# Delta net of a fused two-block network: diagonal blocks gathered by GpSimd, the convolution's last tap on ScalarE, value tiles between the inverse's levels, another entry

## The chip, the cores and the metric

The kernel runs on one core of a Trainium2 chip. The metric is the device time of one execution in microseconds (us); three runs of the kernel before gave 2810.44, 2818.19 and 2819.06, median 2818.19. The engines are TensorE (PE in the profile), VectorE (DVE), ScalarE (ACT), GpSimd (POOL) and SyncE (SP, which only issues the weight transfers here). Each has its own instruction queue and they meet at semaphores. TensorE writes to PSUM, eight banks of 128x512 float32 values.

## The reference, cut to what matters

The network has a first block (two attention layers), and a second one: a feed-forward layer, a mixer and another feed-forward layer, all on 512 tokens of width 1024 in float32. The mixer has two branches. The change concerns one of them, the gated delta net, with 8 query/key heads, 16 value heads, width 128, in chunks:

```
qkv = silu(causal_short_conv(concat([gq, gk, gv]), conv_w))    # 4 taps along the tokens
q_g = l2norm(cq) * 128 ** -0.5;  k_g = l2norm(ck)               # repeated for 2 value heads each
beta = sigmoid(gb);  g = -exp(a_log) * softplus(ga + dt_bias);  gam = cumsum(g)
A  = where(strict, (beta k) k^T * exp(gam_t - gam_s), 0)
T  = inverse(I + A)                                             # unit lower triangular
qk = q k^T * exp(gam_t - gam_s)                                 # t >= s
per chunk:  v_new = T (beta v) - T (beta k exp(gam)) S
            o = (q exp(gam)) S + qk v_new
            S = S exp(g_end) + k_to_end^T v_new
o_g = rmsnorm(o) * silu(gz)
```

## The kernel before, in words

The kernel is a hand-written program: for each engine a Python function issues instructions in a fixed order, and explicit semaphore waits tie the queues together. Nothing reorders them. The delta net works in four groups `g` of two query/key heads and four value heads. A token tile `j` (four of 128 tokens) and a value head give one of 16 units of a group, for which a 128x128 unit triangular matrix is inverted.

Per group there are two parts. `pe_gdn_prepare` and its namesakes on the other engines take the norms of q and k (`sums`: matmuls with one column of output, L2301), scale them (`scale`, L2310), form decays (`diff`, L2348) and products (`kq`, L2323 and L2324), and turn the value tiles 0 and 1 (`v_tok`, a transposition, L386). VectorE forms `lower` (A) and `qk` in four steps j (L3044 to L3057), convolves value tiles 4 and 5, and then solves the 32x32 diagonal blocks of all 16 units at once. For that it copies the blocks with four transposes (L3086), one for each band of 32 partitions, into `bm`, eliminates in 31 steps of two instructions (L3095, L3097), and turns the result back (L3099 gives `block`, L3101 `block_t`). Then it convolves the tiles 6 and 7.

`pe_gdn_inverse_and_state` builds the 128x128 inverse from the solved blocks in two levels: `x5` (L2360), `t5` and `r5` (L2370, L2376) for the 64 level, `x6` (L2385) and `r6` (L2395) for the 128 level, each evicted in halves by ScalarE and VectorE. GpSimd places the diagonal blocks into `tt` and `rr` (L3181, L3185). Value tiles 2 and 3 are turned behind `x5` and behind `r5`. Then come four steps of the state: `ks` and `qs` (L2413, L2418), `vn` (L2430, evicted as `v_new` by ScalarE, L2733), `su` (L2438) and `do` (L2444).

Between all this, TensorE takes steps of a `fill` stream: projections that do not depend on the group, one matmul of 512 columns a step, eight steps a tile, four tiles of `gv`, of `gz` and of the next `gqk` for each group (L2216 and L2234). Each float32 matmul appears as two records in the trace. The fill uses the banks 6 and 7 in turn (`FILL_BANKS`); a bank is free again when ScalarE has copied the tile out. `LEAD` = 12 steps are taken ahead of a group.

A convolution of 4 taps along tokens goes tile by tile. ScalarE copies the projection from PSUM into `pad` behind three zero columns (`act_gdn_pad`, L2615), VectorE multiplies by tap 0 and adds taps 1, 2 and 3 (`dve_gdn_conv`: L3005, L3008 twice, L3010) into `acc`, ScalarE applies Silu (L2628). Both buffers are double, so pad `c` waits for convolution `c - 2`.

At the entry TensorE projects the first `gqk` into `HIGH_BANKS` (4 to 7), computes `gam` (L2259 to L2261), and starts the fill. VectorE zeroes `rr` and `tt` (2048 and 1024 columns, L2983 and L2986) and reduces the identity to `halves` (L2984) before its first convolution. ScalarE does the four Squares (L2637) after the last Silu.

## Time and profile before

| | |
|---|---|
| median of 3 runs | 2818.19 us (2810.44 to 2819.06) |
| profiled execution, its own time | 2815.83 us |
| its span, first to last instruction | 2814.0 us |
| PE busy | 2725.4 us |
| DVE busy | 1305.1 us |
| ACT busy | 620.5 us |
| POOL busy | 28.9 us |
| mean granted TensorE clock | 0.979 |

The delta net lies between about 1654 and 2234 us, in four groups of some 135 us. PE is busy when at least one matmul is under way; the ends of matmuls are modelled, so successive rows overlap by 0.1 to 0.2 us, and the distance from one row's start to the next's is the better price. "Idle before" in square brackets is the time that an engine stood before an instruction, and the name behind the arrow the instruction that released it. The granted clock is a share of 2.4 GHz; 0.5 is 1.2 GHz.

### The profile page before, as it was taken

Reading aid. Unit: us, or ns where it says so; the run is one execution under the profiler, and the core shown is the slowest. Engines: PE = TensorE matmul, PEld = TensorE weight load, DVE = VectorE, ACT = ScalarE, POOL = GpSimd, SP = SyncE. Lnnn points to the kernel's source line nnn. Section 1 sums busy time; section 2 is a strip of 40 time slices with the busy share of each in tenths; the row PEclk is TensorE's granted clock in tenths of the full one; section 3 lists DMA queues with packets and bytes.
Section 4 is the critical chain, followed back from the end, with each engine's and each line's share of the span. In section 5 each row is a group of like instructions: output and inputs, shape, how many; then the busy total and the mean of one; then the engine's idle time right before and its main releaser. Section 6 shows DMA issues by size and latency. Waiting matters only on the chain.

```text
span 2814.0 us, 29186 instructions
## 1 busy us (share of the span) xinstructions
PE 2725.4 (97%) x11644; PEld 1820.0 (65%) x11644; DVE 1305.1 (46%) x2545; ACT 620.5 (22%) x1428; POOL 28.9 (1%) x49
## 2 busy tenths in 40 slices
PE   8999899999999999999999989999999999999999
PEld 5445557656478888746555845646565685688886
DVE  3723333445234456335364427475756362344564
ACT  2122321346200000223333022424232201100001
POOL 0000000000000000000000000000000000000000
...
DMA packets 122478, 195.16 MB, mean 69 GB/s; under 512 B 7212, under 2 KB 63336, under 8 KB 121448
## 3 DMA queue, kind: packets, MB, share of 16 engines
...
q14 instruction: 41, 0.34, 0.0%
...
## 4 chain that ended last, share of the span: by engine, by line
PE 88%; DVE 8%; issue 1%; ACT 1%; DMA 1%; ACTq 0%; DVEq 0%; SPq 0%
PE psum L503 19%; PE psum L500 14%; PE psum L2234 10%; PE psum L413 9%; PE psum L433 8%; PE psum L2216 6%; PE psum L398 6%; PE psum L1137 2%; PE psum L2097 2%; PE psum L1157 2%; DVE arena L3097 1%; DVE arena L3095 1%; PE psum L631 1%; PE psum L1145 1%; PE psum L386 1%
## 5 line engine op out<-in xcount | busy, mean ns | idle before, releaser
L2234 PE MATMUL psum<-weight_ring,h_t 128*128 128x512 f32 x896 | 408.1, 598 | 0.5 <-issue 0.5
L556 DVE TENSOR_TENSOR arena<-arena,psum 128x512 f32<-128x512 f32 x179 | 122.8, 686 | 337.1 <-PE psum L503 287.7
L2234 PEld LDWEIGHTS psum<-weight_ring,h_t 128*128 128x128 f32 x896 | 162.7, 191 | 163.3 <-issue 162.1
L413 PE MATMUL psum<-h_t,weight_ring 128*128 128x512 f32 x560 | 246.7, 601 | 7.7 <-DMA weight_ring<-in_w_in_dram 4.0
L2216 PE MATMUL psum<-h_t,weight_ring 128*128 128x512 f32 x512 | 244.7, 621 | 8.4 <-ACT arena L2615 8.1
L503 PE MATMUL psum<-h_t,weight_ring 128*128 128x256 f32 x1024 | 228.2, 379 | 0.0
L500 PE MATMUL psum<-weight_ring,arena 128*128 128x256 f32 x992 | 220.2, 379 | 1.5 <-ACT arena L2647 1.5
L503 PEld LDWEIGHTS psum<-h_t,weight_ring 128*128 128x128 f32 x1024 | 194.5, 190 | 27.5 <-issue 1.3
L500 PEld LDWEIGHTS psum<-weight_ring,arena 128*128 128x128 f32 x992 | 188.4, 190 | 27.7 <-issue 2.2
L413 PEld LDWEIGHTS psum<-h_t,weight_ring 128*128 128x128 f32 x560 | 107.2, 193 | 142.7 <-issue 134.5
L398 PE MATMUL psum<-weight_ring,h_t 128*128 128x512 f32 (+3 forms) x512 | 182.9, 513 | 0.8 <-DVEq L1583 0.8
L433 PE MATMUL psum<-weight_ring,h_t 128*128 128x512 f32 x384 | 171.3, 608 | 3.3 <-ACT h_t L1224 2.0
L2216 PEld LDWEIGHTS psum<-h_t,weight_ring 128*128 128x128 f32 x512 | 97.4, 200 | 106.8 <-issue 105.6
L500 PE MATMUL psum<-arena 128*128 128x256 f32 x712 | 158.7, 379 | 0.0
L503 PE MATMUL psum<-arena 128*128 128x256 f32 x704 | 155.5, 379 | 0.0
L500 PEld LDWEIGHTS psum<-arena 128*128 128x128 f32 x712 | 135.3, 190 | 18.4
L398 PEld LDWEIGHTS psum<-weight_ring,h_t 128*128 128x128 f32 x512 | 92.8, 207 | 82.7 <-issue 81.6
L503 PEld LDWEIGHTS psum<-arena 128*128 128x128 f32 x704 | 133.8, 190 | 18.2
L433 PEld LDWEIGHTS psum<-weight_ring,h_t 128*128 128x128 f32 x384 | 74.5, 195 | 96.5 <-issue 94.9
L990 ACT ACTIVATE arena<-arena 128x1024 f32<-128x1024 f32 x20 | 21.2, 1058 | 421.3 <-DVE arena L556 421.3
L1173 ACT ACTIVATE arena<-arena,statistics 128x128 f32<-128x128 f32 (+1 forms) x96 | 53.9, 562 | 231.5 <-DVE statistics L1202 231.4
L503 PE MATMUL psum<-arena,weight_ring 128*128 128x256 f32 x384 | 86.8, 379 | 0.0
...
## 6 DMA issues: line engine op xcount, KB each, us to landing
...
```

Of the source, the lines that this page charges most:

```text
L398: last = pe.matmul(bank[:, 0:n_cols], act[:, k0 + k, t * P:(t + 1) * P], slot[:, k, col:col + n_cols], start=(k == 0), stop=(k == nk - 1))
L413: last = pe.matmul(bank, slot[:, k, c:c + P], act[:, k, :], start=(k == 0), stop=(k == KD - 1))
L433: last = pe.matmul(bank, act[:, k0 + k, t * P:(t + 1) * P], slot[:, k, :], start=(k == 0), stop=(k == nk - 1))
L500: ins = pe.matmul(out, right[:, k, q * P:(q + 1) * P], left[:, k, :], start=first, stop=last)
L503: ins = pe.matmul(out, w, right[:, k, :], start=first, stop=last)
L556: ins = dve.tensor_tensor(out, other, bank, op)
L1137: pe.matmul(bank[:, 0:k.shape[-1]], q, k, start=True, stop=True).then_inc(K.full_of((tag, "s", m)), 1)
L1157: last = pe.matmul(bank[:, 0:v.shape[-1]], probs_t[:, i % 2, kb * P:(kb + 1) * P], v, start=(kb == 0), stop=(kb == nkb - 1))
L1173: act.activation(probs[:, n % 2, 0:nk], masked[:, n % 2, 0:nk], ACT.Exp, bias=K.stat[:, 20 + n % 4:21 + n % 4], scale=steps[n]["scale"], a ...
L2097: last = pe.matmul(bank[:, j * P:(j + 1) * P], left[:, c], right[:, c], start=True, stop=True)
L2216: last = pe.matmul(bank, slot[:, k, n * P:(n + 1) * P], act[:, k, :], start=(k == 0), stop=(k == KD - 1))
L2234: last = pe.matmul(bank, act[:, k, t * P:(t + 1) * P], slot[:, k, :], start=(k == 0), stop=(k == KD - 1))
```

## The change

- The diagonal blocks are first copied side by side into a new tile `diag` by GpSimd, 16 copies of 32x128 per group, four for each step j as soon as `lower` of that step is there. VectorE then turns them with one transpose over 128 partitions.
- ScalarE writes the last tap, `w3 * x`, straight from PSUM into `acc`, with a second instruction behind the copy into `pad`; only then is the bank free. It must also wait for the Silu that read `acc` before. VectorE adds the taps 0, 1 and 2. The order of the sums changes with it.
- The value tiles 6 and 7 are convolved behind VectorE's evictions of `x5` and `r5`, their Silus follow on ScalarE, and their transposition stands behind `x6` and `r6` on TensorE.
- At the entry `gqk` goes into banks 0 to 3 and `gam` into bank 4; the fill's first lead is 16 steps instead of 12, and four fewer come before the value tiles of group 0. GpSimd zeroes `rr` and `tt`, the reduction to `halves` moves to the setup, and ScalarE does each Square right behind its Silu.

Two new semaphores carry the gather (`lower_ready`, `blocks_gathered`), one (`delta_entered`) the memset of the pads.

```diff
@@ -859,2 +862,3 @@
     dve.wait_ge(K.ident_landed, 16)
+    dve.tensor_reduce(K.halves[:], K.const("ident").rearrange("p (q h c) -> p h q c", q=4, h=2), AX.XY, ALU.add).then_inc(K.one_more("dve"), 1)
     for t in range(NT):
@@ -2053,4 +2057,5 @@
     e = serial
-    for name, n in (("bm", 1024), ("bt", 512), ("bx", 256)):
+    for name, n in (("bm", 1024), ("bt", 512), ("bx", 256), ("diag", 512)):
         V[name], e = K.carve(e, n)
+    V["diag"] = V["diag"].rearrange("p (u c) -> p u c", c=32)
     V["block"], V["block_t"] = (V["bm"][:, 512 * n:512 * n + 512].rearrange("p (u c) -> p u c", c=32) for n in range(2))
@@ -2139,3 +2144,3 @@
     pe.wait_ge(K.weight_landed[blk % SLOTS], K.landed_at[blk])
-    K.banks_in_turn = HIGH_BANKS
+    K.banks_in_turn = LOW_BANKS
     pe_feature_major(K, pe, (s, "gqk", 0), K.h_t, [0, P, 2 * P, 3 * P], blk)
@@ -2255,5 +2260,6 @@
 def pe_gdn(K, pe, s, V):
-    K.banks_in_turn = WORK_BANKS
+    K.banks_in_turn = SIDE_BANKS
     pe.wait_ge(K.gdn_decays, 1)
     bank = pe_fresh(K, pe, (s, "gam"))
+    K.banks_in_turn = WORK_BANKS
     pe.matmul(bank[:, 0:64], K.const("cum"), V["gd"][:, 0, :], start=True, stop=True)
@@ -2262,3 +2268,3 @@
     fill = pe_gdn_stream(K, pe, s)
-    pe_take(fill, LEAD)
+    pe_take(fill, FIRST_LEAD)
     for g in range(4):
@@ -2273,3 +2279,3 @@
 
-LEAD = 12
+LEAD, FIRST_LEAD = 12, 16
 
@@ -2328,3 +2334,3 @@
         pe_transpose(K, pe, (s, "k_tok", g, m), lambda t, m=m: c_qk[:, 2 + m, t * P:(t + 1) * P])
-    pe_take(fill, 4 * KD - LEAD - 14)
+    pe_take(fill, 4 * KD - (LEAD if g else FIRST_LEAD) - 14)
     for n in range(2):
@@ -2361,3 +2367,2 @@
         last.then_inc(K.full_of((s, "x5", g, p)), 1)
-    pe_gdn_values(K, pe, s, V, g, 2)
     pe_take(fill, 4)
@@ -2377,3 +2382,2 @@
         last.then_inc(K.full_of((s, "r5", g, p)), 1)
-    pe_gdn_values(K, pe, s, V, g, 3)
     pe_take(fill, 4)
@@ -2387,2 +2391,3 @@
         last.then_inc(K.full_of((s, "x6", g, p)), 1)
+    pe_gdn_values(K, pe, s, V, g, 2)
     pe_take(fill, 4)
@@ -2397,2 +2402,3 @@
         last.then_inc(K.full_of((s, "r6", g, p)), 1)
+    pe_gdn_values(K, pe, s, V, g, 3)
     pe_take(fill, 4)
@@ -2578,9 +2584,8 @@
     act.activation(V["gd"][:, 4:7, :].rearrange("p a b -> p (a b)"), bank[:, 0:192], ACT.Exp).then_inc(K.free_of((s, "gam")), 1)
-    for n in range(4):
-        act_gdn_pad(K, act, s, V, 0, n)
+    for n in range(5):
+        if n < 4:
+            act_gdn_pad(K, act, s, V, 0, n)
         if n:
             act_gdn_conv_silu(K, act, s, V, 0, n - 1)
-    act_gdn_conv_silu(K, act, s, V, 0, 3)
-    for n in range(4):
-        act_gdn_square(K, act, s, V, 0, n)
+            act_gdn_square(K, act, s, V, 0, n - 1)
     for g in range(4):
@@ -2614,3 +2619,11 @@
         act.wait_ge(K.conv_done, c - 1)
-    act.copy(V["pad"][:, n % 2, 3:T + 3], K.bank(key)).then_inc(K.free_of(key), 1)
+    act.copy(V["pad"][:, n % 2, 3:T + 3], K.bank(key)).then_inc(K.one_more("act"), 1)
+    if c >= 2:
+        act.wait_ge(K.conv_silu, c - 1)
+    act.activation(V["acc"][:, n % 2, :], K.bank(key), ACT.Copy, scale=conv_tap(K, g, n, 3)).then_inc(K.free_of(key), 1)
+
+
+def conv_tap(K, g, n, i):
+    tile = (2 * g + n, 8 + 2 * g + n - 2)[n >= 2] if n < 4 else 16 + 4 * g + n - 4
+    return K.conv_w[:, 32 * i + tile:32 * i + tile + 1]
 
@@ -2683,4 +2696,2 @@
         act.activation(V["z"][:, n, :], K.bank(((s, "gz", g), n)), ACT.Silu).then_inc(K.free_of(((s, "gz", g), n)), 1)
-    act_gdn_conv_silu(K, act, s, V, g, 6)
-    act_gdn_conv_silu(K, act, s, V, g, 7)
 
@@ -2698,3 +2709,2 @@
     act.copy(V["x5"][32:64].rearrange("p u c -> p (u c)"), K.bank(key)[32:64, :]).then_inc(K.free_of(key), 1)
-    act_gdn_values(K, act, s, V, g, 2)
     key = (s, "t5", g)
@@ -2707,3 +2717,3 @@
                    scale=-1.0).then_inc(K.free_of(key), 1)
-    act_gdn_values(K, act, s, V, g, 3)
+    act_gdn_conv_silu(K, act, s, V, g, 6)
     key = (s, "x6", g, 0)
@@ -2711,2 +2721,4 @@
     act.copy(V["x6"][64:128, 0:8, :].rearrange("p u c -> p (u c)"), K.bank(key)[64:128, :]).then_inc(K.free_of(key), 1)
+    act_gdn_conv_silu(K, act, s, V, g, 7)
+    act_gdn_values(K, act, s, V, g, 2)
     act_gdn_following(K, act, s, V, g, 0)
@@ -2716,2 +2728,3 @@
                    scale=-1.0).then_inc(K.free_of(key), 1)
+    act_gdn_values(K, act, s, V, g, 3)
     act_gdn_keys_to_end(K, act, s, V, g, 0)
@@ -2978,2 +2991,3 @@
     gd = V["gd"]
+    dve.memset(V["pad"][:, :, 0:3], 0.0).then_inc(K.delta_entered, 1)
     dve.wait_ge(K.free_of((s, "gam")), K.turn((s, "gam")))
@@ -2981,8 +2995,3 @@
     dve.tensor_tensor(gd[:, 6, :], gd[:, 6, :], gd[:, 2, :], ALU.mult).then_inc(K.one_more("dve"), 1)
-    dve.memset(V["pad"][:, :, 0:3], 0.0).then_inc(K.one_more("dve"), 1)
-    dve.memset(V["rr"], 0.0).then_inc(K.one_more("dve"), 1)
-    dve.tensor_reduce(K.halves[:], K.const("ident").rearrange("p (q h c) -> p h q c", q=4, h=2), AX.XY, ALU.add).then_inc(K.one_more("dve"), 1)
-    dve.wait_ge(K.steps["dve"], K.step_n["dve"])
-    dve.memset(V["tt"], 0.0).then_inc(K.triangles_zeroed, 1)
-    dve.wait_ge(K.steps["dve"], K.step_n["dve"])
+    dve.wait_ge(K.delta_entered, 1)
     for n in range(4):
@@ -2997,15 +3006,8 @@
     key = ((s, "gqk", g), n) if n < 4 else ((s, "gv", g), n - 4)
-    c = 8 * g + n
     dve.wait_ge(K.free_of(key), K.turn(key))
-    if c >= 2:
-        dve.wait_ge(K.conv_silu, c - 1)
-    tile = (2 * g + n, 8 + 2 * g + n - 2)[n >= 2] if n < 4 else 16 + 4 * g + n - 4
     acc, x = V["acc"][:, n % 2, :], V["pad"][:, n % 2, :]
-    w = lambda i: K.conv_w[:, 32 * i + tile:32 * i + tile + 1]
-    dve.tensor_scalar(acc, x[:, 0:T], w(0), None, ALU.mult).then_inc(K.one_more("dve"), 1)
-    dve.wait_ge(K.steps["dve"], K.step_n["dve"])
-    for i in range(1, 3):
-        dve.scalar_tensor_tensor(acc, x[:, i:T + i], w(i), acc, ALU.mult, ALU.add).then_inc(K.one_more("dve"), 1)
+    for i in range(2):
+        dve.scalar_tensor_tensor(acc, x[:, i:T + i], conv_tap(K, g, n, i), acc, ALU.mult, ALU.add).then_inc(K.one_more("dve"), 1)
         dve.wait_ge(K.steps["dve"], K.step_n["dve"])
-    dve.scalar_tensor_tensor(acc, x[:, 3:T + 3], w(3), acc, ALU.mult, ALU.add).then_inc(K.conv_done, 1)
+    dve.scalar_tensor_tensor(acc, x[:, 2:T + 2], conv_tap(K, g, n, 2), acc, ALU.mult, ALU.add).then_inc(K.conv_done, 1)
 
@@ -3055,3 +3057,3 @@
     ins = dve.tensor_tensor(by_head(V["lower"][:, 4 * j:4 * j + 4, :]), two(0), by_head(decay), ALU.mult)
-    ins.then_inc(K.one_more("dve"), 1)
+    ins.then_inc(K.lower_ready, 1)
     ins = dve.tensor_tensor(by_head(V["qk"][:, 4 * j:4 * j + 4, :]), two(1), by_head(decay), ALU.mult)
@@ -3081,7 +3083,5 @@
     bm, bt = V["bm"], V["bt"]
-    dve.wait_ge(K.steps["dve"], K.step_n["dve"])
-    for b in range(4):
-        rows = slice(32 * b, 32 * b + 32)
-        units = V["lower"][rows, :, rows].rearrange("p u c -> p c u").unsqueeze(2).to_broadcast([32, 32, 2, 4 * NT])
-        dve.transpose(bm[rows, :].rearrange("p (i c) -> p c i", c=32), units).then_inc(K.one_more("dve"), 1)
+    dve.wait_ge(K.blocks_gathered, 16 * (g + 1))
+    units = V["diag"].rearrange("p u c -> p c u").unsqueeze(2).to_broadcast([P, 32, 2, 4 * NT])
+    dve.transpose(bm.rearrange("p (i c) -> p c i", c=32), units).then_inc(K.one_more("dve"), 1)
     dve.wait_ge(K.steps["dve"], K.step_n["dve"])
@@ -3101,4 +3101,2 @@
     dve.transpose(V["block_t"], V["block"]).then_inc(K.blocks_solved, 1)
-    dve_gdn_conv(K, dve, s, V, g, 6)
-    dve_gdn_conv(K, dve, s, V, g, 7)
 
@@ -3110,2 +3108,3 @@
     dve.tensor_copy(V["x5"][96:128].rearrange("p u c -> p (u c)"), K.bank(key)[96:128, :]).then_inc(K.free_of(key), 1)
+    dve_gdn_conv(K, dve, s, V, g, 6)
     key = (s, "r5", g, 1)
@@ -3114,2 +3113,3 @@
                       ALU.mult).then_inc(K.free_of(key), 1)
+    dve_gdn_conv(K, dve, s, V, g, 7)
     key = (s, "x6", g, 1)
@@ -3167,3 +3167,6 @@
 def pool_gdn(K, pool, V):
-    pool.wait_ge(K.triangles_zeroed, 1)
+    pool.wait_ge(K.delta_entered, 1)
+    pool.memset(V["rr"], 0.0).then_inc(K.triangles_zeroed, 1)
+    pool.memset(V["tt"], 0.0).then_inc(K.triangles_zeroed, 1)
+    pool.wait_ge(K.triangles_zeroed, 2)
     for g in range(4):
@@ -3177,2 +3180,8 @@
             pool.tensor_copy(V["bt"][:, 256 * h:256 * (h + 1):17], ones).then_inc(K.identity_set, 1)
+        pool.wait_ge(K.identity_set, 3 * (g + 1))
+        for j in range(NT):
+            pool.wait_ge(K.lower_ready, NT * g + j + 1)
+            for b in range(4):
+                rows, units = slice(32 * b, 32 * b + 32), slice(4 * j, 4 * j + 4)
+                pool.tensor_copy(V["diag"][rows, units, :], V["lower"][rows, units, rows]).then_inc(K.blocks_gathered, 1)
         pool.wait_ge(K.blocks_solved, 2 * g + 1)
```

TensorE's queue at the entry and at the first inverse, before (L2216 and L2234 are the fill, L2301 the sums, L386 transpositions, L2360 `x5`, L2370 and L2376 `t5` and `r5`, L2385 `x6`, L2395 `r6`; a count is of matmuls):

```order
L2261 MATMUL psum<-arena,consts_sb 128x64
L2216 MATMUL psum<-h_t,weight_ring 128x512 x12
L2301 MATMUL psum<-consts_sb,arena 128x1 x16
...
L2216 MATMUL psum<-h_t,weight_ring 128x512 x6
L386 MATMUL psum<-consts_sb,arena 128x128 x8
L2234 MATMUL psum<-weight_ring,h_t 128x512 x32
L2360 MATMUL psum<-arena 32x32 x32
L386 MATMUL psum<-consts_sb,arena 128x128 x4
L2216 MATMUL psum<-h_t,weight_ring 128x512 x4
L2370 MATMUL psum<-arena 32x32 x16
L2376 MATMUL psum<-arena 32x32 x32
L386 MATMUL psum<-consts_sb,arena 128x128 x4
```

The same places of the changed kernel, whose line numbers are a few higher (L2221 and L2239 the fill, L2307 the sums, L389 transpositions, L2366 `x5`, L2375 and L2381 `t5` and `r5`, L2389 `x6`, L2400 `r6`):

```order
L2267 MATMUL psum<-arena,consts_sb 128x64
L2221 MATMUL psum<-h_t,weight_ring 128x512 x16
L2307 MATMUL psum<-consts_sb,arena 128x1 x16
...
L2366 MATMUL psum<-arena 32x32 x32
L2221 MATMUL psum<-h_t,weight_ring 128x512 x4
L2375 MATMUL psum<-arena 32x32 x16
L2381 MATMUL psum<-arena 32x32 x32
L2221 MATMUL psum<-h_t,weight_ring 128x512 x4
L2389 MATMUL psum<-arena 64x64 x16
L389 MATMUL psum<-consts_sb,arena 128x128 x4
L2221 MATMUL psum<-h_t,weight_ring 128x512 x4
L2400 MATMUL psum<-arena 64x64 x16
L389 MATMUL psum<-consts_sb,arena 128x128 x4
```

The lead is four steps longer, and each of the two transpositions of four has moved down behind the next level. VectorE's queue from the end of the elimination to the first eviction behind `r6`, before (L3099 and L3101 the transposes that end it, L3110, L3113, L3117 and L3120 the evictions of `x5`, `r5`, `x6` and `r6`):

```order
L3099 STREAM_TRANSPOSE arena<-arena 128x16x2x16
L3101 STREAM_TRANSPOSE arena<-arena 128x512
L3005 TENSOR_SCALAR arena<-arena,conv_columns 128x512
L3008 SCALAR_TENSOR_TENSOR arena<-arena,conv_columns 128x512 x2
L3010 SCALAR_TENSOR_TENSOR arena<-arena,conv_columns 128x512
L3005 TENSOR_SCALAR arena<-arena,conv_columns 128x512
L3008 SCALAR_TENSOR_TENSOR arena<-arena,conv_columns 128x512 x2
L3010 SCALAR_TENSOR_TENSOR arena<-arena,conv_columns 128x512
L3110 COPY arena<-psum 32x512
L3113 TENSOR_SCALAR arena<-psum 32x16x32
L3117 COPY arena<-psum 64x512
L3120 TENSOR_SCALAR arena<-psum 64x8x64
```

And of the changed kernel (L3010 and L3012 are now the taps, L3108 and L3112 the evictions of `x5` and `r5`):

```order
L3099 STREAM_TRANSPOSE arena<-arena 128x16x2x16
L3101 STREAM_TRANSPOSE arena<-arena 128x512
L3108 COPY arena<-psum 32x512
L3010 SCALAR_TENSOR_TENSOR arena<-arena,conv_columns 128x512 x2
L3012 SCALAR_TENSOR_TENSOR arena<-arena,conv_columns 128x512
L3112 TENSOR_SCALAR arena<-psum 32x16x32
L3010 SCALAR_TENSOR_TENSOR arena<-arena,conv_columns 128x512 x2
L3012 SCALAR_TENSOR_TENSOR arena<-arena,conv_columns 128x512
L3117 COPY arena<-psum 64x512
L3120 TENSOR_SCALAR arena<-psum 64x8x64
```

The convolutions of tiles 6 and 7 stand one behind each of the first two evictions, and each is three instructions instead of four.

## Rows read from the trace of the kernel before

**Rows 1.** The page: its span, and TensorE's and the others' busy time.

```profile
span 2814.0 us, 29186 instructions
PE 2725.4 (97%) x11644; PEld 1820.0 (65%) x11644; DVE 1305.1 (46%) x2545; ACT 620.5 (22%) x1428; POOL 28.9 (1%) x49
```

**Rows 2.** TensorE's waits, 1640 to 2240 us: total us, times, longest us.

```profile
PE psum L386 <- ACT arena L2628: 10.7, 8, 2.7
PE psum L2360 <- DVE arena L3099: 8.9, 4, 2.2
PE psum L2216 <- ACT arena L2615: 8.1, 1, 8.1
PE psum L2438 <- ACT arena L2733: 2.7, 3, 0.9
PE psum L2444 <- ACT arena L2733: 0.9, 3, 0.3
```

**Rows 3.** Windows: length, busy us of each engine, granted clock, DMA share, GB/s.

```profile
1654.10:1662.70 8.60, 0.45 (x5) 0.34 (x4) 6.98 (x13) 3.68 (x6) 1.15 (x3) 0.78 0.00 0
1662.70:1667.00 4.30, 4.30 (x7) 1.97 (x8) 4.16 (x7) 1.19 (x3) 0.00 (x0) 0.65 0.26 58
1678.10:1683.40 5.30, 5.30 (x11) 2.26 (x11) 0.43 (x2) 2.03 (x3) 0.00 (x0) 0.68 0.00 0
1744.40:1747.20 2.80, 2.80 (x7) 1.77 (x8) 2.66 (x5) 0.15 (x1) 0.50 (x1) 0.50 0.00 0
1873.50:1886.40 12.90, 8.21 (x79) 5.05 (x79) 9.92 (x16) 3.02 (x5) 5.02 (x6) 0.74 0.14 41
2146.30:2159.30 13.00, 8.12 (x77) 4.88 (x78) 9.91 (x16) 3.02 (x5) 5.02 (x6) 0.74 0.15 44
```

**Rows 4.** Timeline of TensorE at the entry: start, length, count [idle before].

```profile
1662.63 12.08 PE L2216 MATMUL psum<-h_t,weight_ring 128*128 128x512 f32 x24 [8.15 <-ACT arena L2615]
1674.55 3.63 PE L2301 MATMUL psum<-consts_sb,arena 128*128 128x1 f32 x32
1678.04 5.38 PE L2216 MATMUL psum<-h_t,weight_ring 128*128 128x512 f32 x8
```

**Rows 5.** Timeline of TensorE, group 0's value tiles and inverse.

```profile
1709.22 0.66 PE L386 MATMUL psum<-consts_sb,arena 128*128 128x128 f32 x4 [0.18 <-ACT arena L2628]
...
1739.58 2.61 PE L2360 MATMUL psum<-arena 32*32 32x32 f32 x64 [2.23 <-DVE arena L3099]
...
1750.01 1.10 PE L2370 MATMUL psum<-arena 32*32 32x32 f32 x29
...
1752.96 0.66 PE L386 MATMUL psum<-consts_sb,arena 128*128 128x128 f32 x4
...
1756.98 2.08 PE L2385 MATMUL psum<-arena 64*64 64x64 f32 x32
```

**Rows 6.** Timeline of VectorE: convolution 5, the transposes, convolution 6.

```profile
1705.66 0.48 DVE L3005 TENSOR_SCALAR arena<-arena,conv_columns 128x512 f32<-128x512 f32 x1
1706.17 1.54 DVE L3008 SCALAR_TENSOR_TENSOR arena<-arena,conv_columns 128x512 f32<-128x512 f32 x2
...
1708.42 8.00 DVE L3086 STREAM_TRANSPOSE arena<-arena 32x1024 f32<-32x1024 f32 x4
...
1738.46 1.06 DVE L3099 STREAM_TRANSPOSE arena<-arena 128x512 f32<-128x512 f32 x1
...
1740.67 1.99 DVE L3008 SCALAR_TENSOR_TENSOR arena<-arena,conv_columns 128x512 f32<-128x512 f32 x2
```

**Rows 7.** Timeline of GpSimd, group 0.

```profile
1658.76 0.69 POOL L3173 MEMSET arena<- 128x512 f32 x1 [44.16 <-DVE arena L2986]
1659.51 0.46 POOL L3177 COPY arena<-block_halves 128x16 f32<-128x16 f32 x2
...
1741.16 3.73 POOL L3185 COPY arena<-arena 32x512 f32<-32x512 f32 x4
```

**Rows 8.** Timeline of ScalarE: four scaled copies out of PSUM.

```profile
1823.58 2.42 ACT L2647 ACTIVATE arena<-psum,gain_columns 128x512 f32<-128x512 f32 x4 [10.22 <-PE psum L386]
```

3 lines of the change are left out of this document (added).

## The prediction

> **What bounds the kernel now.** I read the page's busy times first. TensorE (PE) is busy for 2725.4 of the 2814.0 us of the span; VectorE (DVE), next, for less than half of it [rows 1]. So the order of the work decides nothing in most of the kernel, and a change to other engines pays only where PE stands. The second view is therefore PE's waits in the stretch from 1640 to 2240 us, the delta net, the only place that the diff touches beside one instruction of the setup [rows 2]. The reader is to see five kinds. PE waits once 8.1 us for ScalarE's (ACT) copies L2615, at the entry. It waits four times, 8.9 us together, for VectorE's L3099, the end of the serial elimination; eight times, 10.7 us together, for the Silu L2628 of a value tile; six times, 2.7 and 0.9 us together, for L2733 in the state. That is 31.3 us, about 1.1% of the span.
>
> The third view, windows, shows that the waits cost more than their length. In the entry's wait the granted clock is 0.78 and in the 4.3 us behind it 0.65; in the 2.8 us behind the wait for a value tile it is 0.50, so TensorE is at 1.2 GHz there instead of 2.4. The whole stretch from the end of the fill to the second level of the inverse runs at 0.74 in every later group [rows 3]. One fall has another origin: behind the 32 one-column matmuls of the sums, where PE was busy, the clock is 0.68 too, and this change leaves that as it is.
>
> **Entry.** Before, `gq/gk` lay in banks 4 to 7 and the fill needs 6 and 7, so it waited for copies of tiles 2 and 3, which wait for VectorE's convolutions; those began after 3072 columns of memset. Afterwards the banks differ, the fill begins at once, and its first 16 tiles' steps (32 records) run at full clock. A step of two records costs 0.86 us: from 1752.96 to 1756.98 lie 4 transpose records (0.50 us) and 8 of the fill, 3.52 us [rows 5]. The lead ends at 1654.5 + 16 x 0.86 = 1668.2. Are the squares ready for the sums by then? ACT makes four passes of 512 columns per tile (copy, scaled copy, Silu, Square), each taken at the 0.6 us of a scaled copy [rows 8]: 2.4. VectorE does three taps of 0.77 (1706.17 to 1708.42 are three, [rows 6]): 2.3. Two copies, the first conv, three more tiles at ACT's pace and the last Silu and Square give 1.2 + 2.3 + 7.2 + 1.2 = 11.9 behind `gam`, 1666.4. So the sums start near 1668.2 instead of 1674.6 [rows 4], with four more fill steps done.
>
> Two waits are new in group 0. The fill's third tile wants bank 6, free only after pad 4, which ACT does after the square root of the sums: two copies at 0.6 and about 0.2 for the root, 1.4 us of PE idle. And the four steps of fill (3.4 us) that were taken early are missing before the value tiles, where VectorE's chain of products and two convs is the later one: the second value transposition stood at 1709.2 behind a wait of 0.18 [rows 5]. It moves by -6.4 + 1.4 = -5.0 with the sums, by -1.0 with the two shorter convs (below), by +2.0 with the contention (below): -4.0. PE comes there 8.4 us earlier, so it stands some 4.4 us in front of the tiles 0 and 1, and I add 1.0 for the clock, two thirds of what the entry's wait cost in this way (0.35 of 4.3 us). Entry and preparation of group 0: **3.0 us gained**, out of 8.1 + 1.5 that the old wait cost.
>
> **Elimination and value tiles.** Four 32-partition transposes take 8.00 us; one over 128 partitions of 1024 columns should take 2.0 (L3099 moves half as many in 1.06): 6.0 less [rows 6]. Each conv loses its tensor_scalar, 0.48 and a step, 0.52. So the blocks are solved 7.0 us earlier against the products, less the contention, where PE waited 2.2: at a contention of 2.0 a slack of 2.8 is left, 3.8 with PE itself 1.0 later (below). The two waits for value tiles 2 and 3 go as well, since they now stand behind x6 and r6. Conv 6 follows at once on the eviction of x5, ends 5.1 us after PE's end of fill, and its transposition comes at 14. Conv 7 ends at 11.5, is wanted at 20. (Counted in PE's own records: x5 2.0, fill 3.5, t5 and r5 3.0, fill 3.5, x6 2.0 and so on, and 0.7 for an eviction, 2.3 for a conv.) ACT has a scaled copy of 0.6 more per pad; where v_new of the first state step waits behind it, the trace shows no wait of PE today, and I count it as hidden (rival 4 is that it is not).
>
> Price: from the end of the fill to L2370 were 1750.01 - (1739.58 - 2.23) = 12.66 us in group 0 [rows 5], 12.9 and 13.0 in groups 1 and 3 (the last two windows of [rows 3]; by starts of rows 12.8, 12.9 and 13.0 in groups 1 to 3), together 51.4. What is left: 64 records of x5 at 96 in 2.95 us (1750.01 to 1752.96), 1.97, fill 3.52 and the moved transposes 0.50: 5.99. **Gain 51.4 - 24.0 = 27.5 us.** 18.9 us of this is waiting (8.9, and 10.7 without the four waits of 0.18, [rows 2]), the rest clock.
>
> **State.** L2733 held PE by 0.9 and 0.3 us in each of groups 0 to 2, behind a conv on VectorE. A conv shorter by 0.52 leaves 0.4: 3 x 0.8 = **2.4 us gained**.
>
> **The gather.** Sixteen GpSimd (POOL) copies of 32x128 per group run beside VectorE's products and convs 4, 5. No row shows that shape. Time of one: between a 128x16 copy, 0.23 us, and a 32x512 one, 0.93 [rows 7]; 16 take 3.7 to 14.9 us, and the last four, 0.9 to 3.7, fit in the two convs (4.5), so VectorE does not wait for the gather. What it costs VectorE: beside the 32x512 copies a tap took 0.99 us instead of 0.77 [rows 6, 7], some 0.24 per GpSimd copy. So 16 copies cost from 0 to 3.8 us; the copies being a quarter as long, I take 2.0. With convs 1.03 shorter, the value tiles 0 and 1 of groups 1 to 3 are waited for 0.18 - 1.03 + 2.0 = 1.15 us instead of 0.18: **2.9 us lost**. The upper end, 3.8, loses 5.4 more in these three groups and 1.8 in group 0.
>
> The Trainium skill (SBUF — State Buffer, "Who interferes with whom") says that a VectorE instruction with two SBUF inputs contends with a GpSimd instruction that reads SBUF, and that whoever comes first holds the shared ports for its whole instruction. The trace agrees with the sign (0.99 against 0.77) but not with full blocking by a copy of 0.93. By the page most of the products, which have two SBUF inputs, would stand behind each copy in full, 3.7 us per group at the 0.23 of the shortest row; this speaks for the first rival.
>
> Moved at no price: the halves' reduction lies in the setup, where VectorE waits for the first rows; POOL's memsets of 3072 columns (512 take 0.69, [rows 7], so about 4 us) are done 60 us before use; they can stretch the entry's convs by some 1 us, inside its slack of 1.8.
>
> **Sum.** 3.0 + 27.5 + 2.4 - 2.9 = 30.0 us off the profiled execution's 2815.8 (a span of 2814.0 and 1.8 around it): 2785.8. The median shown is 2.4 us above that execution: 2788.
>
> **Rivals.**
> 1. Contention at its upper end. For it: the stretched taps. Against: short copies. It gives 7.2 us back, and waits of 3 us bring the clock down in front of the long fill, about 1 us in each of three groups: 2798. Chance 0.18.
> 2. The clock does not come back. x5 is 2 us of 32x32 matmuls, t5 and r5 3 more; after the one-column sums the clock fell with PE busy (0.68, rows 3). For it: that fall. Against: L2370 and L2376 took 2.95 us for 96 records without one. If it falls behind x5, some 2 us per group, 8 together: 2796. Chance 0.12.
> 3. VectorE is not slowed, and group 0 goes without its clock price: 2.9 + 0.5 (the old waits of 0.18) + 2.0 + 1.0 less: 2782. For it: the copies are a quarter as long as those of rows 7. Against: there are 16. Chance 0.12.
> 4. The waits move rather than go: ACT, with 32 more instructions, becomes late at v_new or at the pads that free banks 6 and 7, by 0.7 us and more at two or three places per group, with the clock down each time: 6 us x 4 come back, 2812. For it: L2733 has waits now [rows 2]. Against: ACT is the least busy of the three. Chance 0.06.
> 5. The other side: the gather is late. It counts when the 16 copies end more than 3.8 us behind conv 5, some 20 us after the first `lower`, from 1.25 us per copy; at 2.4 us each (GpSimd waiting for VectorE in each copy) they end 22 behind it, and PE stands 18.4 us and about 1 for the clock per group: 78 us on top of the forecast, 2866. No row of POOL is near that. Chance 0.04.
>
> The forecast as worked out, 2783 to 2794, has 0.48. With the rivals next to it the range is 2777 to 2804. A change is told from none here from about 0.3%, 8.5 us: faster 0.90, same 0.06, slower 0.04.
>
> **What would show it.** Right: no wait for L2615 at the entry; none for the end of the elimination; in the stretch behind the fill a clock near 1.0 and about 6 us; one transpose of 2.0 us; a PE wait of 1 to 2 us behind the first sums and one of some 4 us at its first value tiles; products stretched by about 2 us. Wrong: a clock of 0.5 behind x5, waits for value tiles of 3 us in every group, or POOL copies of over 1.2 us with VectorE waiting for them.

## The result and the profile after

The changed kernel takes 2774.98 us (median of 4 runs, 2772.54 to 2776.67), beside 2817.99 for the kernel before on the same chip (4 runs, 2810.44 to 2819.06). The ratio is 0.9852, 95% interval 0.9833 to 0.9871: 1.5% faster. The prediction was 2788 with 2777 to 2804; the kernel is 13 us faster than that and 2 below the range. The profiled execution took 2772.54 us, 43.3 less than the one of before (2815.83). Of this, 1.9 us lies ahead of the delta net (`gam` starts at 1651.84 instead of 1653.71, with nothing but the banks of `gqk` changed there for TensorE), and **41.3 us** in it: from `gam` to the first matmul behind the last state it is 542.02 us instead of 583.36, where 30.0 had been worked out. This distance is called the delta net's length below.

The page, its first lines:

```profile
span 2770.7 us, 29212 instructions
PE 2708.6 (98%) x11644; PEld 1812.8 (65%) x11644; DVE 1260.6 (45%) x2499; ACT 638.8 (23%) x1460; POOL 59.6 (2%) x115
```

Against [rows 1] PE has the same 11644 records and is busy for 16.8 us less, although it does the same work: this part of the gain is clock. ScalarE (ACT) has 18 us more to do, GpSimd (POOL) 31. PE's waits from 1640 to 2240 us (total us, times, longest):

```profile
PE psum L389 <- ACT arena L2641: 2.5, 2, 1.6
PE psum L503 <- ACT arena L2660: 1.5, 1, 1.5
PE psum L2221 <- ACT arena L2623: 1.4, 1, 1.4
PE psum L2444 <- ACT arena L2746: 1.1, 3, 0.4
```

Of the kinds in [rows 2] the wait for L3099 is gone, and the waits for value tiles (L389 for L2641) are two instead of eight, both in group 0. All waits between `gam` and the first matmul behind the last state sum to 6.6 us instead of 32.9; both sums hold the same 1.5 us behind the last state, which [rows 2] does not show. So 26.3 us of the 41.3 is waiting, and the other 15.0 is put down to the clock. TensorE's timeline of group 0 and of the sums of group 1 (start, length, count, idle before):

```profile
1652.45 13.95 PE L2221 MATMUL psum<-h_t,weight_ring 128*128 128x512 f32 x32
1666.24 3.63 PE L2307 MATMUL psum<-consts_sb,arena 128*128 128x1 f32 x32
...
1671.30 6.69 PE L2221 MATMUL psum<-h_t,weight_ring 128*128 128x512 f32 x8 [1.43 <-ACT arena L2623]
...
1700.70 0.66 PE L389 MATMUL psum<-consts_sb,arena 128*128 128x128 f32 x4 [0.95 <-ACT arena L2641]
...
1702.91 0.66 PE L389 MATMUL psum<-consts_sb,arena 128*128 128x128 f32 x4 [1.55 <-ACT arena L2641]
...
1730.96 2.11 PE L2366 MATMUL psum<-arena 32*32 32x32 f32 x64
1733.00 3.70 PE L2221 MATMUL psum<-h_t,weight_ring 128*128 128x512 f32 x8
1736.63 1.10 PE L2375 MATMUL psum<-arena 32*32 32x32 f32 x29
...
1794.93 3.63 PE L2307 MATMUL psum<-consts_sb,arena 128*128 128x1 f32 x32
1798.42 3.68 PE L2221 MATMUL psum<-h_t,weight_ring 128*128 128x512 f32 x8
1801.93 3.73 PE L2316 MATMUL psum<-consts_sb,arena 128*128 128x128 f32 x32
```

The entry has no wait ([rows 4] has 8.15), and the inverse none ([rows 5] has 2.23): from the start of `x5` to `t5` it is 5.67 us. The last three rows are the surprise. Eight fill records behind the one-column sums take 3.51 us from start to start; before they took 5.21 (from 1678.04 in [rows 4] to 1683.25, the start of `scale`). Windows (length, busy us of each engine, granted clock, DMA share, GB/s):

```profile
1671.30:1677.80 6.50, 6.50 (x8) 2.71 (x9) 0.00 (x0) 1.25 (x1) 0.00 (x0) 0.53 0.00 0
1798.40:1803.60 5.20, 5.20 (x25) 3.29 (x25) 4.63 (x19) 1.34 (x3) 0.00 (x0) 1.00 0.01 3
1864.00:1873.00 9.00, 9.00 (x117) 6.22 (x113) 3.64 (x5) 3.65 (x7) 0.00 (x0) 1.00 0.41 155
```

Behind the first sums the clock is down (0.53), more than in [rows 3] (0.68), and here PE had also waited 1.43 us. Behind the sums of group 1 it is 1.00, and so it is up to the end of the delta net; the kernel before fell behind the sums in all four groups. The third window holds group 1's `x5`, fill, `t5` and `r5`, at 1.00 where [rows 3] has 0.74. VectorE and GpSimd in group 0:

```profile
1694.27 0.69 DVE L3059 TENSOR_TENSOR arena<-arena 128x512 f32<-128x512 f32 x1
1694.87 0.78 DVE L3046 TENSOR_TENSOR arena<-arena 128x512 f32<-128x512 f32 x1
...
1697.56 1.57 DVE L3010 SCALAR_TENSOR_TENSOR arena<-arena,conv_columns 128x512 f32<-128x512 f32 x2
...
1702.10 2.08 DVE L3086 STREAM_TRANSPOSE arena<-arena 128x1024 f32<-128x1024 f32 x1
...
1726.26 1.08 DVE L3099 STREAM_TRANSPOSE arena<-arena 128x512 f32<-128x512 f32 x1
```

```profile
1687.86 2.00 POOL L3186 COPY arena<-arena 32x128 f32<-32x128 f32 x4 [57.18 <-DVE arena L3057]
...
1697.11 2.97 POOL L3186 COPY arena<-arena 32x128 f32<-32x128 f32 x4 [0.62 <-DVE arena L3057]
```

One transpose takes 2.08 us where four took 8.00 [rows 6]. Four gather copies take 2.0 to 2.1 us beside the products, and the last four of each group 2.97, beside the taps of convolution 4 (all 64: 527 ns on average). On VectorE one product grows from 0.69 to 0.78 and nothing else by more than 0.03. Where a tap and a small copy meet, it is the copy that grows, by some 0.24 us each, and GpSimd's time is off the path here.

### The profile page after: what moved, and what is told of

It is laid out like the page before. It is cut to its first block, busy times and chain, and to the rows that moved or that the text cites. A ratio compares the mean times of both kernels' runs of the same rounds, so it can differ in the third digit from the quotient of the medians.

```text
span 2770.7 us, 29212 instructions
## 1 busy us (share of the span) xinstructions
PE 2708.6 (98%) x11644; PEld 1812.8 (65%) x11644; DVE 1260.6 (45%) x2499; ACT 638.8 (23%) x1460; POOL 59.6 (2%) x115
## 4 chain that ended last, share of the span: by engine, by line
PE 95%; DVE 2%; ACT 1%; DMA 1%; issue 1%; ACTq 0%; DVEq 0%; SPq 0%
PE psum L506 19%; PE psum L503 14%; PE psum L2239 14%; PE psum L416 9%; PE psum L436 8%; PE psum L2221 7%; PE psum L401 6%; PE psum L1141 2%; PE psum L2102 2%; PE psum L1161 2%; PE psum L634 1%; PE psum L389 1%; PE psum L1149 1%; PE psum L2450 1%; PE psum L2316 1%
## 5 line engine op out<-in xcount | busy, mean ns | idle before, releaser
L2239 PE MATMUL psum<-weight_ring,h_t 128*128 128x512 f32 x896 | 406.6, 596 | 0.5 <-issue 0.5
L2239 PEld LDWEIGHTS psum<-weight_ring,h_t 128*128 128x128 f32 x896 | 162.0, 191 | 162.3 <-issue 161.1
L416 PE MATMUL psum<-h_t,weight_ring 128*128 128x512 f32 x560 | 245.7, 599 | 7.9 <-DMA weight_ring<-in_w_in_dram 4.2
L2221 PE MATMUL psum<-h_t,weight_ring 128*128 128x512 f32 x512 | 235.4, 601 | 1.7 <-ACT arena L2623 1.4
L2221 PEld LDWEIGHTS psum<-h_t,weight_ring 128*128 128x128 f32 x512 | 93.6, 192 | 94.0 <-issue 91.5
```

Of the source, the lines that this page charges most:

```text
L416: last = pe.matmul(bank, slot[:, k, c:c + P], act[:, k, :], start=(k == 0), stop=(k == KD - 1))
L2221: last = pe.matmul(bank, slot[:, k, n * P:(n + 1) * P], act[:, k, :], start=(k == 0), stop=(k == KD - 1))
L2239: last = pe.matmul(bank, act[:, k, t * P:(t + 1) * P], slot[:, k, :], start=(k == 0), stop=(k == KD - 1))
```

## The experiments

The gain is larger than the forecast by 11 us in the delta net. The theory: the contention of the sixteen small copies is near zero (3.4 us of waiting in groups 1 to 3, about 2 in group 0), and the clock falls behind the sums are gone in three groups (1.7 us each). Its rivals: the falls come at moments of the chip's own, whatever the kernel does, so that the 5 us are chance; and a copy costs VectorE the same whatever its size, the gain being elsewhere. All medians below are of runs beside runs of the kernel before on the same chip.

**Again.** The kernel before and the changed one unchanged, once each, and the changed one timed later.

> The kernel before, unchanged, a second profile. In the first, the granted clock fell behind the one-column sums in all four groups: the 8 fill records behind them took 5.2 us from start to start instead of 3.5 (1.7 us each). Theory A (the fall belongs to the order of the work: it needs the waits of 0.9 and 0.3 us in the state steps ahead of the sums, and group 0 its own): four falls again, 5.2 us each, profiled time within 2813 to 2819. Theory B (it is chance how the sums meet the clock's own timing, equal for groups of equal length): falls in another number of groups, possibly none, and the profiled time shorter by 1.7 us for each missing one, down to 2810.

> The changed kernel, unchanged, a second profile. In the first, the clock fell behind the sums in group 0 only (6.5 us with a wait of 1.4 ahead) and stayed full in groups 1 to 3 (3.5 us). Theory A: the same again, profiled time 2772 to 2775. Theory B: falls in some of the groups 1 to 3, and a time up to 5 us longer. Contention of GpSimd's copies is the same in any case: the products of a group take 12.0 us from the first L3046 to the first tap, as in the kernel before.

> The changed kernel on the same chip as the next one: 2772 to 2777, and one of three profiles alike (falls in group 0 only). If timing decides, single runs of up to 2786 can appear, as with the two added matmuls.

2816.37 and 2772.63 us. The first has the delta net at 583.36 again and falls behind all four sums, the second at 542.07 with a fall in group 0 alone. Timed: 2774.84 (four runs), 0.9861 (0.9845 to 0.9878); one of its runs is 2781.55, at a mean clock of 0.984 instead of 0.987. So the missing falls are no accident of one execution: the third trace (2772.77 us) has them missing too. Whether the slower runs had them is not shown, since only the first run of each set has a trace. The three traces are also alike in another way: their `gam` starts at 1651.84, 1651.94 and 1652.16, so they are no three independent cases.

### The parts

**Only the gather.** The hunks of `diag`, `lower_ready` and `blocks_gathered` on the kernel before:

```diff
-        dve.transpose(bm[rows, :]..., units)   # four, 32 partitions each
+    dve.wait_ge(K.blocks_gathered, 16 * (g + 1))
+    dve.transpose(bm..., units)                # one, 128 partitions
```

> The kernel before with only GpSimd's gather and the one transpose. The blocks are solved 6.0 us earlier, so the four waits of 2.2 us for L3099 go; the value tiles 2 and 3 stay behind x5 and r5, but convs 6 and 7, right behind the elimination, are early too, so the waits of 2.2 to 2.7 us for their Silu go as well. From the end of gz's fill to t5: 12.7 to 13.0 us before, 6.0 to 6.5 expected here (1.97 + 3.5 + 0.5): 4 x 6.7 = 27 us faster, 2788. If GpSimd's copies cost VectorE 2 us a group (as predicted), waits for value tile 1 of 2.2 us (0.18 before) in each group: 2795; if 0.1 (as the first trace suggests), of 0.3: 2788. Rival 'values': the second wait needs the moved value tiles, and stays at 2 us: 2800.

2789.48 (2785.62 to 2791.35), ratio 0.991 (0.9894 to 0.9927), as expected; delta net 553.19. No wait for L3099 is left:

```profile
PE psum L2220 <- ACT arena L2619: 8.1, 1, 8.1
...
PE psum L2442 <- ACT arena L2737: 2.7, 3, 0.9
...
PE psum L389 <- ACT arena L2632: 1.2, 4, 0.3
```

This run measures the contention directly: the wait for the second value tile, 0.18 in [rows 5], is 0.31 four times. The gather costs it 0.13 us per group, not 2.0. It takes the waits for tiles 2 and 3 too, since these hung on VectorE, late for the same reason. Its clock behind the four sums:

```profile
1674.50:1683.30 8.80, 8.80 (x57) 6.81 (x56) 1.05 (x3) 2.03 (x3) 0.00 (x0) 1.00 0.00 0
1800.70:1809.50 8.80, 8.80 (x57) 6.83 (x56) 4.70 (x19) 2.65 (x7) 0.00 (x0) 1.00 0.01 2
1928.60:1937.40 8.80, 8.80 (x42) 5.78 (x41) 4.64 (x19) 2.68 (x7) 0.00 (x0) 0.81 0.00 0
2058.20:2067.00 8.80, 8.80 (x41) 5.70 (x40) 4.64 (x19) 2.71 (x7) 0.00 (x0) 0.81 0.00 0
```

The same instructions in the same order, in one execution, with PE busy throughout: no fall in groups 0 and 1, a fall in 2 and 3. What differs is the time: the sums start 126.2, 127.9 and 129.6 us after those of the group before.

**All but the gather.** The same hunks left out of the changed kernel.

> The changed kernel with the four 32-partition transposes on VectorE instead of the gather. The blocks were solved some 3.5 us before PE wanted them; 6.0 us later they are 2.5 us late, so a wait for L3099 of 2.0 to 2.5 us in groups 0 to 3 and the clock down behind x5: 3.5 us each, 14 us slower than the changed kernel, 2787 to 2791. Rival (the moved convolutions alone would have sufficed): no wait, 2775.

2790.51 (2783.09 to 2792.12), 0.9908 (0.9891 to 0.9924), as expected; delta net 559.04.

```profile
PE psum L2365 <- DVE arena L3100: 7.0, 4, 2.2
PE psum L389 <- ACT arena L2640: 2.3, 2, 1.4
```

The moved value tiles and the shorter convolutions do not reach the wait at the end of the elimination: it is there, 7.0 of 8.9 us. The gather is needed, worth 15.7 us here (against 2774.84) and 26.4 alone.

**Only the value tiles' new place; only the last tap on ACT; only the entry.**

```diff
-    pe_gdn_values(K, pe, s, V, g, 2)      # behind x5, now behind x6; 3 from r5 to r6
+    act.activation(V["acc"][:, n % 2, :], K.bank(key), ACT.Copy, scale=conv_tap(K, g, n, 3))
-LEAD = 12
+LEAD, FIRST_LEAD = 12, 16                 # with the banks, memsets, halves and Squares
```

> The kernel before with only the value tiles 6 and 7 and their transpositions moved. The elimination still ends 2.2 us late, so the wait of 2.2 us for L3099 stays and the clock falls behind it as before; the wait for the Silu of tile 2 (2.2 to 2.7 us, four times) goes. Four times 2.4 us and part of the clock: 10 to 14 us faster, 2801 to 2805. Rival 'gather suffices' (the two waits have one cause): same reading here, since this tests only whether the second wait goes by itself; if it is replaced by a wait behind x6 or r6, under 4 us.

> The kernel before with only the last tap on ScalarE. Elimination 1.03 us earlier: the wait for L3099 falls from 2.2 to 1.2, that for the Silu from 2.2 to about 1.2 (another conv 0.5 shorter, the ScalarE copy early), value tile 1 without wait, the state's waits from 1.2 to 0.4: 1.0 + 0.5 + 0.2 + 0.8 = 2.5 us in groups 0 to 2, less in 3, 9 us, and some clock if the shorter waits let it stay: 2801 to 2806. Rival: ScalarE's 32 more instructions (18 us) become late somewhere: a new wait for ScalarE, gain under 4 us.

> The kernel before with only the entry changed: banks, lead 16, memsets on GpSimd, halves in the setup, each Square behind its Silu. The convolution keeps four VectorE instructions, so an entry tile takes 2.8 us there and the squares are ready some 2 us later than with three. From gam to the start of gz's fill (56.0 us before, 51.6 in the changed kernel): I expect 53 to 54, since VectorE's convs 4 and 5 are 1.0 longer and nothing else differs; 2 to 3 us gained, 2812 to 2816 against 2815. Rival: the whole gain of 4.4 us belongs to the entry alone (the convs do not matter): 51.6.

2805.66 (0.997, 0.996 to 0.9979), 2805.24 (0.9963, 0.9947 to 0.998) and 2811.18 (0.9987, 0.9978 to 0.9997), each within 1 us of its forecast. The first removes the waits for value tiles 2 and 3 but keeps the four of 2.2 us for the elimination; the second shortens these to 1.6 and the four for tiles 2 and 3 from 10.0 to 7.9 us; the third has no wait of 8.1 us and one of 0.8 for a bank. In it `gam` to the fill of `gz` is 50.9 us, below the 53 to 54 expected and even below the changed kernel's 51.6; its first fall is half as long (at 0.50 for 3 us, not 6). With 26.4 for the gather the parts sum to 4.7 + 26.4 + 10.2 + 10.6 = 51.9 us, more than the 43 of the whole: the gather and the new place each take away the same waits for tiles 2 and 3, and the tap shortens them. How much of the overlap is falls of the clock, which come or stay away differently in each part, is not separated.

### The contention: four large copies instead of sixteen small

```diff
-        for j in range(NT):
-            pool.wait_ge(K.lower_ready, NT * g + j + 1)
-            for b in range(4):
-                pool.tensor_copy(V["diag"][rows, units, :], V["lower"][rows, units, rows])...
+        pool.wait_ge(K.lower_ready, NT * (g + 1))
+        for b in range(4):
+            pool.tensor_copy(V["diag"][rows, :, :], V["lower"][rows, :, rows])...
```

> The changed kernel with the gather in 4 copies of 32x512 per group, issued when the last lower tile is there, instead of 16 of 32x128. They run beside the qk product and convs 4 and 5. Theory 'size': a copy of 512 columns holds up VectorE where one of 128 does not; each copy takes 0.8 to 0.95 us and stretches about one tap by 0.2 us, 0.8 us per group; the copies end 3.6 us behind the last lower tile and are hidden by the convs (4.5 us); a wait for value tile 1 of some 0.5 us per group. Theory 'neighbour' (the stretched taps of before had another cause, the Silu and copies of ScalarE beside them): taps of 0.77, copies of 0.65. Time within 2 us of the changed kernel in both, unless the clock falls elsewhere.

2784.38 (2781.82 to 2785.24), 0.989 (0.9876 to 0.9903), not within the 2 us expected. GpSimd and VectorE in group 0, and all copies of the two kinds:

```profile
1701.24 3.98 POOL L3185 COPY arena<-arena 32x512 f32<-32x512 f32 x4 [66.37 <-DVE arena L3057]
```

```profile
1701.62 2.11 DVE L3010 SCALAR_TENSOR_TENSOR arena<-arena,conv_columns 128x512 f32<-128x512 f32 x2
...
1707.26 2.06 DVE L3086 STREAM_TRANSPOSE arena<-arena 128x1024 f32<-128x1024 f32 x1
```

```profile
L3185 POOL COPY arena<-arena 32x512 f32<-32x512 f32 x16 | 15.3, 953 | 99.5 <-DVE arena L3057 98.8
...
L3193 POOL COPY arena<-arena 32x512 f32<-32x512 f32 x16 | 9.7, 607 | 0.9
```

Two taps take 2.11 us beside large copies, 1.57 beside small ones: four copies stand beside the taps in both kernels, so this compares the size alone. Convolutions 4 and 5 take 5.64 us (1701.62 to 1707.26) instead of 4.54 (1697.56 to 1702.10), 1.1 more: 0.27 per copy, as the 0.24 of the prediction had it for this shape. The copy itself takes 953 ns beside them, 607 without. The wait for the first value tiles is then 0.30 us in groups 1 to 3; the prediction's formula gives 0.18 - 1.03 + 1.1 = 0.25. So formula and price per large copy are right, and the rival of an equal price per copy is out: sixteen small copies cost less than these four. The profiled execution is 11.7 us longer than the changed kernel's (9.5 at the medians). Of this, 4.1 us lies ahead of `gam` (1655.98), 1.9 is waiting, all for value tiles, and most of the rest is three more falls of the clock to 0.50 for 3 us: behind the value tiles and behind `r5` of group 0, and behind the sums of group 1, which this edit does not touch.

### The clock behind the narrow matmuls

**A shorter lead.** It takes group 0's waits away and shifts all that follows.

```diff
-LEAD, FIRST_LEAD = 12, 16
+LEAD, FIRST_LEAD = 12, 12      # the second kernel: 12, 14
```

> The changed kernel with a first lead of 12 fill steps instead of 16, so 6 steps instead of 2 ahead of the value tiles of group 0. The three waits of group 0 (1.43 us for the third tile's bank, 0.95 and 1.55 us for the value tiles) came from the four steps taken early. Theory 'lead': all three go, and with them the fall of the clock behind the first wait is shorter or gone: 4 to 6 us faster than the changed kernel, 2769 to 2771. The squares were ready 1.5 us before the sums at a lead of 16; at 12 the sums start 3.4 us earlier and their last tile is ready just in time. Rival: the entry needs 16 steps; a wait for the squares of up to 2 us appears instead and the gain is under 2 us.

> The changed kernel with a first lead of 14 fill steps. Two steps of the second tile are left behind the sums and cover 1.7 us, so the wait of 1.43 us for bank 6 goes; the value tiles are reached 1.7 us later, so of 0.95 and 1.55 us there some 0.8 is left. Theory 'lead': 2.5 to 4.5 us faster than the changed kernel, 1 to 2 us slower than a lead of 12. Rival (squares are late at 12, not at 14): faster than a lead of 12.

2781.15 (2778.02 to 2781.82), 0.9881 (0.9864 to 0.9898), and 2781.31 (2780.09 to 2784.32), 0.9882 (0.9865 to 0.9899). Both were expected to be faster than the changed kernel, and both are 6 us slower at the median. The first has 2.65 us of waits instead of 6.6, yet its delta net is 546.24, 4.2 us longer; its `gam` also starts 5.1 us later (1656.95), ahead of the edit. Behind the sums, and over `x5` to `r5`, of group 1:

```profile
1797.70:1802.90 5.20, 5.20 (x10) 2.20 (x10) 4.64 (x19) 1.34 (x3) 0.00 (x0) 0.67 0.01 3
1863.00:1872.00 9.00, 9.00 (x107) 5.20 (x105) 3.44 (x5) 1.69 (x3) 0.00 (x0) 0.81 0.62 228
```

Eight fill records behind the sums cost 1.77 us more in every group, and 1.8 more behind `r5` in the last three; groups 1 and 2 take 129.7 us from sums to sums, where the changed kernel takes 126.3. Nothing is different in groups 1 to 3 but when they happen. This is the prediction's second rival, absent in the changed kernel and there in its near twin.

**The sums spread.** One fill step behind each head's eight one-column records instead of four behind all, in the kernel before and in the changed kernel with a lead of 12.

```diff
-    last.then_inc(K.full_of((s, "sums", g)), 1)
-    pe_take(fill, 4)
+        if n == 3:
+            last.then_inc(K.full_of((s, "sums", g)), 1)
+        pe_take(fill, 1)
```

> The kernel before with only the sums spread as above. Its two profiles had four falls behind the sums. Theory 'low activity': none now, 4 x 1.7 = 6.8 us faster, 2808 to 2811. Rival 'timing only': as before, 2813 to 2818.

> The changed kernel with a first lead of 12 and the sums spread: one fill step behind each head's four one-column matmuls instead of four steps behind all sixteen. With lead 12 alone the clock fell twice per group, behind the sums (1.7 us) and behind t5 and r5 (1.7 us), and the time was 2781. Theory 'low activity': a fall needs a stretch of few or narrow matmuls with PE busy, and here the one at the sums is gone: no fall behind the sums in any group, the fill and sums together 7.0 us; the fall behind t5 and r5 may stay. 2781 - 4 x 1.7 = 2774, or 2768 if the other goes by chance. Rival 'timing only': it is where in time the work stands that decides, not how dense it is: falls behind the sums remain, 2781.

2811.61 (2802.58 to 2814.37, 10 runs), 0.9989 (0.9979 to 0.9998), so 3.4 us faster where 6.8 had been expected, and 2773.9 (2771.1 to 2774.2), 0.9857 (0.9844 to 0.987). TensorE at the first sums of the kernel before, spread:

```profile
1676.11 0.95 PE L2301 MATMUL psum<-consts_sb,arena 128*128 128x1 f32 x8
1676.91 1.10 PE L2216 MATMUL psum<-h_t,weight_ring 128*128 128x512 f32 x2
```

And the clock over the same stretch:

```profile
1674.50:1682.00 7.50, 7.50 (x46) 5.34 (x45) 0.42 (x2) 1.39 (x3) 0.00 (x0) 1.00 0.00 0
```

Two fill records take 0.95 us with the turn (1676.91 to 1677.86, the start of the next sums), and no fall is left behind any sums, in either kernel. In the kernel before, 7.1 us of falls went and 4.1 us of the delta net with them; the stretch from `x5` to `t5` behind the wait for the elimination grew in groups 0, 1 and 3 (in group 1 from 10.63 to 11.70 us), a deeper fall of the clock. With a lead of 12, 7.5 us of the delta net came back (538.76 instead of 546.24), with two falls left, both behind `r5`. So an unbroken stretch of one-column matmuls is a condition of the fall behind the sums. Over all traces of this case the clock falls in or behind the unbroken sums in 37 of 56 groups (14 traces), and behind the broken ones in 0 of 16 (4 traces). The groups of one execution are not independent draws, as they follow one another at nearly equal distances (126.3 us in the changed kernel, 129.7 with a lead of 12, some 136.4 before from group 1 on): if one falls, the next mostly does too.

**All narrow stretches broken up**, also `x5`, `t5` and `r5`, one fill step behind each half of `x5` and `r5` and behind `t5`.

```diff
         last.then_inc(K.full_of((s, "x5", g, p)), 1)
-    pe_take(fill, 4)
+        pe_take(fill, 1)
+    pe_take(fill, 2)
```

> Lead 12, sums spread, and the four steps behind x5 and the four behind r5 spread between the halves of x5, behind t5 and between the halves of r5. Theory 'low activity': no fall anywhere in the groups; group length 126.3 us for all, as in the changed kernel's profile; 2781 - 4 x 1.7 - 3 or 4 x 1.7 = 2767 to 2769. Rival 'timing only': some falls remain and the time stays over 2774. Evictions of x5 and r5 start up to 0.9 us later; if one becomes late, a wait for it of under 1 us shows in each group.

> Lead 12 with the fill spread between narrow matmuls, on the same chip: 2769 to 2772, so 4 to 6 us below the changed kernel, with a spread of under 4 us between runs, since no stretch of narrow matmuls is left for the clock to fall in. Rival: the difference seen across calls was chance; equal within 2 us.

2769.72 (2768.99 to 2772.51), 0.9846 (0.9832 to 0.9859), the second time 2775.17 (2770.93 to 2775.64), 0.9851 (0.9838 to 0.9865), beside 2774.84 for the changed kernel. Its granted clock is 1.00 over the whole delta net in both traces, and it has these waits alone:

```profile
PE psum L503 <- ACT arena L2664: 1.5, 1, 1.5
PE psum L2448 <- ACT arena L2750: 1.1, 3, 0.4
```

Yet its groups 1 and 2 take 127.8 us instead of the 126.3 expected: the broken order itself costs 1.5 us a group. The second time it missed its forecast of 2769 to 2772. The two medians, 5.5 us apart, differ in the traced executions by where `gam` starts, 1651.8 and 1656.1, ahead of all edits; the delta net is 540.35 and 540.38. The five runs of the second set lie in two clusters, 2770.93 and 2771.05, and 2775.17 to 2775.64, about as far apart as the two starts of `gam`. No version is shown to beat the changed kernel.

**Two matmuls ahead.** The changed kernel with two more matmuls, 1.7 us, ahead of `gam`.

```diff
+    for _ in range(2):
+        pe.matmul(bank, K.const("ones"), K.const("causal"), start=True, stop=True)
```

> The changed kernel with two more 512-column matmuls (four records, 1.7 us of TensorE, results overwritten) ahead of gam, nothing else. Theory 'timing': the delta net is the same work 1.7 us later against the clock's own timing; falls behind the sums or behind r5 appear in groups 1 to 3, and the time grows by more than the 1.7 us, up to 2774 + 1.7 + 6 x 1.7 = 2786. Rival: the absence of falls belongs to the order of work of the changed kernel: 2776 to 2777 and no falls in groups 1 to 3.

2782.96 (2777.03 to 2789.34), 0.9891 (0.9874 to 0.9908). The profiled execution, 2778.46, is 5.9 us longer than the changed kernel's: 1.7 for the two matmuls, 3.0 ahead of them (they start at 1654.84, `gam` at 1656.55), and 1.3 in the delta net, 543.29 us. That part is one more fall, behind the value tiles of group 0:

```profile
1707.50:1710.80 3.30, 3.30 (x8) 1.73 (x6) 2.99 (x10) 1.66 (x4) 0.00 (x0) 0.50 0.01 2
```

The falls expected in groups 1 to 3 did not come in this execution, so its trace speaks for the rival. The other four run from 2777 to 2789 at mean clocks of 0.981 to 0.986, a spread of 12 us where the changed kernel's first four had 4. An edit of 1.7 us costs 8 at the median. That the rest is falls is inferred from the clocks; those runs have no trace.

## Why the prediction was wrong in its size

**Right.** The place and the mechanism. The entry's wait is gone, the sums start 14.4 us behind `gam` (forecast 14.5), the new wait for bank 6 is 1.43 us (1.4), that for `v_new` 0.4 (0.4). The transpose takes 2.08 us (2.0); the blocks are solved at 1727.34, 3.6 us before PE wants them (2.8 to 3.8). The inverse: gains of 7.5 forecast for group 0 with its state, 7.7 found. Entry and preparation of group 0: 4.4 found for 3.0, with 1.9 of waiting less than forecast and a deeper fall of the clock against it (0.53 in the first window). Rivals 4 and 5 did not come: no wait of PE is released by ACT's added 18 us or POOL's 31, apart from those forecast.

**The first failed step: "16 copies cost from 0 to 3.8 us; the copies being a quarter as long, I take 2.0."** It was 0.1 us per group. The sixteen products of group 0 with their gaps, from the first one's start to the start of convolution 4, took 11.82 us before (1691.07 to 1702.89) and 11.92 after (1685.64 to 1697.56); convolutions 4 and 5 took 4.54, where six taps at 754 ns, the mean of all L3010, are 4.5. Three waits of 1.15 us did not come, and in group 0 PE stood 0.95 + 1.55 = 2.5 us instead of some 4.4: 5.4 us of waiting together. The nearest row was a copy four times as wide, and I scaled by count and length as if contention were proportional to GpSimd's time. The four large copies show the row's own price holds (1.1 us for four), and the small copies that it does not carry over. Why a small copy gives way to a tap, growing from some 0.50 to 0.74 us itself, where a large one takes from it, no run here shows.

The Trainium skill (SBUF — State Buffer, "Who interferes with whom") has a two-input VectorE instruction contend with a GpSimd instruction that reads SBUF. Here that shows in every second step of four products, in one of them, by 0.09 us, in the small copies beside the taps, and beside large copies in the taps, which take 1.05 us. The page calls the shared ports an exclusive lock; that whoever comes second is blocked for a whole instruction it says of VectorE's two-port modes, and such blocking is in no row here: a product would have grown by the 0.5 us of a copy.

**The second failed step: the fall behind the sums, "and this change leaves that as it is."** It left in three groups of four: L2307 to L2316 is 7.0 us instead of 8.7, 1.7 x 3 = 5.1 us. I had taken a fall that stood in four groups of one trace for a property of the stretch. The runs show it to be a property of the stretch and of the moment. Broken up, it falls in none of 16 groups; unbroken, in 4 of 4 groups (before, leads of 12 and 14), in 2 of 4 (the gather alone), in 1 (the changed kernel). The Trainium skill (TensorE: Matmul & The Clock Gate, "What's actually happening") calls its window of activity free-running, not tied to the program; the four stretches of the gather alone agree, and no run here can show the window itself. So the rival of chance holds in part: the 5 us of the clock are an outcome that an equal kernel may miss, as the lead of 14 does. They came in all three traced executions of the changed kernel; its other runs can be judged by their mean clock alone (0.984 to 0.987).

The two steps explain 5.4 + 5.1 = 10.5 of the 11.3 us between 41.3 and 30.0. From `x5` to `t5` another 1.3 came in (5.67 us four times where 5.99 was worked out), and the deeper fall in group 0 took some 0.5 back. The other 1.9 us of the profiled difference lies ahead of the delta net. It was not forecast and no run shows its cause; equal kernels differ there by 0.1 to 4.3 us from trace to trace. So the median lies below the range in part by luck: by this and by the 5.1. Rival 3 of the prediction, 2782, had the contention at nothing, which came, and group 0 without its price for the clock, which did not; no rival had the falls behind the sums go.

One reading of the prediction is slightly off and changes nothing: eight fill records in 3.52 us make 0.88 us a step there, not 0.86, which other rows give (13.79 us for sixteen steps from 1652.45 on).

**Open** is why the falls come just where they do: which moment of the chip's decides could not be read from these traces.
